# Two attention stages of a one-core transformer kernel: the output projection joined to the sparse attention, and single instructions moved up in the delta-rule stage

## What is computed

```
return jnp.concatenate([o, m], axis=-1) @ w_out        # second layer: o sparse attention, m memory attention
...
sol = lax.linalg.triangular_solve(lhs, rhs, left_side=True, lower=True, unit_diagonal=True)
u, w = sol[..., :Dv], sol[..., Dv:]
...
v_new = u_i - jnp.einsum('bhcd,bhde->bhce', w_i, S)    # per chunk of the delta rule, S is the state
...
z = jnp.einsum('bqhd,bkhd->bhqk', q[:, start:end], k[:, :end]).astype(jnp.float32) * scale
...
tail = lax.cumsum(log_one_minus, axis=3, reverse=True) - log_one_minus
A = jnp.where(strict, jnp.exp(log_beta + tail), 0.0)   # stick-breaking
```

## Time and profile before

| what | us |
|---|---|
| median of 3 runs (1991.64 to 1992.54) | 1992.03 |
| time of the profiled execution | 1987.48 |
| its span in the trace | 1985.8 |
| PE busy, 10461 matmuls | 1920.5 |
| DVE busy | 1125.8 |
| ACT busy | 731.7 |
| POOL busy | 181.7 |

### The profile page before, as it was taken

One profiled execution on the slowest core, in us unless ns is written; L12 is line 12 of the kernel. 1 busy time (PEld: TensorE's weight loads), 2 busy tenths in 40 slices (PEclk: granted clock), 3 DMA queues, 4 the chain that ended last, 5 costly groups with the idle time before them and its releaser, 6 DMA issues. The chain is left out here.

```text
span 1985.8 us, 27212 instructions
## 1 busy us (share of the span) xinstructions
PE 1920.5 (97%) x10461; PEld 1574.5 (79%) x10461; DVE 1125.8 (57%) x1633; ACT 731.7 (37%) x1152; POOL 181.7 (9%) x179
## 2 busy tenths in 40 slices
PE   8999999999999998999999999999988999999998
PEld 7788788888788876668888878888777788888786
DVE  6435565566435547735665553558655567777533
ACT  7442542222324436624222232424643442222322
POOL 2201020000002004401000000200141020000001
PEclk9999999999999999999999999999999999999999
DMA  7311223332323520023323322242010223322331
GB/s 240 126 45 44 75 85 100 102 95 85 106 96 82 142 80 1 1 85 106 96 85 106 98 93 95 65 117 85 11 44 2 83 77 102 110 85 85 106 96 43
DMA packets 138567, 167.73 MB, mean 84 GB/s; under 512 B 28354, under 2 KB 106727, under 8 KB 138471
## 3 DMA queue, kind: packets, MB, share of 16 engines
q1 hardware_dynamic: 138291, 166.37, 27.3%
q10 hardware_dynamic: 180, 0.05, 0.0%
HBM read 164.29 MB, written 2.10 MB: 84 GB/s over the span
## 5 line engine op out<-in xcount | busy, mean ns | idle before, releaser
L195 PE MATMUL bank<-h_hi,w_hi 128*128 128x512 f32 x2192 | 860.1, 392 | 15.1 <-DVE h_lo L1666 6.3
L196 PE MATMUL bank<-h_lo,w_hi 128*128 128x512 f32 x2192 | 853.8, 390 | 0.0
L197 PE MATMUL bank<-h_hi,w_lo 128*128 128x512 f32 x2192 | 853.7, 389 | 0.0
L142 DVE TENSOR_TENSOR w_lo<-raw,w_hi 128x1024 fp32r<-128x1024 f32 x274 | 334.4, 1236 | 561.0 <-ACT w_hi L136 560.6
L195 PEld LDWEIGHTS bank<-h_hi,w_hi 128*128 128x128 f32 x2192 | 411.8, 188 | 109.5 <-issue 13.9
L136 ACT CAST w_hi<-raw 128x1024 fp32r<-128x1024 f32 x274 | 283.9, 1047 | 575.8 <-PE bank L195 569.2
L197 PEld LDWEIGHTS bank<-h_hi,w_lo 128*128 128x128 f32 x2192 | 411.9, 188 | 86.3
L196 PEld LDWEIGHTS bank<-h_lo,w_hi 128*128 128x128 f32 x2192 | 412.0, 188 | 85.9 <-issue 2.2
L1562 ACT ACTIVATE scratch<-scratch 128x512 f32<-128x512 f32 x66 | 41.8, 633 | 250.8 <-DVE scratch L1627 250.8
L326 POOL TENSOR_TENSOR tail<-keep 128x512 f32<-128x512 f32 x7 | 9.8, 1395 | 1209.7 <-ACT keep L310 1193.6
L1627 DVE SCALAR_TENSOR_TENSOR scratch<-keep,vecs,scratch 128x512 f32<-128x512 f32 x88 | 66.2, 752 | 10.8 <-DVE scratch L1626 1.7
(11 more groups left out here) (466 smaller groups left out, 1832.0 us busy)
## 6 DMA issues: line engine op xcount, KB each, us to landing
raw<-in_w_up SPq DMA_DIRECT2D x176, 256.0 KB, 3.0
raw<-in_w_down SPq DMA_DIRECT2D x44, 512.0 KB, 3.2
raw<-in_w_ffn_up SPq DMA_DIRECT2D x88, 256.0 KB, 3.3
raw<-in_w_mix_in SPq DMA_DIRECT2D x24, 512.0 KB, 3.7
raw<-in_w_ffn_down SPq DMA_DIRECT2D x22, 512.0 KB, 3.5
raw<-in_w_mem_kv SPq DMA_DIRECT2D x16, 512.0 KB, 5.0
raw<-in_a_w_in SPq DMA_DIRECT2D x16, 512.0 KB, 3.7
raw<-in_a_w_out SPq DMA_DIRECT2D x8, 512.0 KB, 3.9
```

The costliest lines, as they stand in the source:

```text
L142: dve.tensor_tensor(k.w_lo[n % RING][:, :], k.raw[n % RING][:, :], k.w_hi[n % RING][:, :].bitcast(F32), ALU.subtract)\
L195: a = pe.matmul(out, sh, mh, start=first, stop=False)
L196: pe.matmul(out, sh, ml, start=False, stop=False)
L197: c = pe.matmul(out, sl, mh, start=False, stop=last)
```

## The change

No product and no elementwise operation is added or left out. Five things stand elsewhere:

1. `stage_out_projection` is gone, and its work stands inside the block of `stage_nsa`. Its first weight chunk (kk 0 and 1, 24 matmuls) stands inside head 3, behind `turn(3, 8)` and `values_sel`; the other three stand behind `values_mem(3)`. SP's loads for it stand in that block, too.
2. In head 0 of the sparse attention the memory scores' `lows(9)` stands behind `weigh_sel(0, 0)` on DVE, and `exps(9)` behind the first `copy_turned` on ACT.
3. In the delta stage `exponents(0, 0)` stands ahead of `softplus(0, 2)` and `softplus(0, 3)`.
4. `weights(0, 3)` stands ahead of `y_copy(8)` on ACT.
5. For the second pair `exponents(1, 0)` stands ahead of `softplus(1, 2)`; `softplus(1, 3)` behind the two instructions that negate the corner of the inverse (L3221); and `exponents(1, 3)` behind the first copy to `vn`.

```diff
-def pe_group(k, pe, t, tiles, h_from=None, aside=None, rstd_by=None, order=tuple(range(8)), bank_free=None):
+def pe_group(k, pe, t, tiles, h_from=None, aside=None, rstd_by=None, order=tuple(range(8)), bank_free=None,
+             ready=None, chunks=range(4)):
...
-            pe.wait_ge(k.h_ready.sem, k.h_ready.at(h_from + order.index(kk) + 1))
+            pe.wait_ge(k.h_ready.sem, k.h_ready.at(h_from + (ready or order).index(kk) + 1))
...
-    for c in range(4):
+    for c in chunks:
...
+    first = k.ring.took
+    ho = k.handoff = Handoff(k, rounded=8)
     with k.nc.Block() as blk:
+        @blk.sync
+        def _(sp):
+            stream(k, sp, first + 8)
+
...
+            def out_bank_free(i):
+                if i == 0:
+                    pe.wait_ge(zc_read, 8)
+                elif i == 2:
+                    pe.wait_ge(me_done, 16)
...
                     elif m == 8:
                         values_sel(j, (2, 3))
+                        if j == 3:
+                            pe_group(k, pe, 0, out_tiles, 0, bank_free=out_bank_free, ready=order, chunks=(0,))
...
             values_mem(3)
+            pe_group(k, pe, 0, out_tiles, 0, ready=order, chunks=(1, 2, 3))
+            pe.wait_ge(fin, 4)
+            pe.wait_ge(finm, 4)
+            pe_group(k, pe, 4, out_tiles)
...
-            for n in range(NB):
+            for n in range(9):
                 lows(n)
                 if n == 5:
                     coef_local(0)
             weigh_sel(0, 0)
+            lows(9)
             weigh_sel(0, 1)
...
+            out_projection_dve(k, dve, ho, gain, first)
...
+                    if j == 0 and m == 0:
+                        exps(9)
...
+            out_projection_act(k, act, ho, gain, first)
...
             weights(0, 2)
+            weights(0, 3)
             y_copy(8)
-            weights(0, 3)
...
             r_step(2, 1)
+            exponents(0, 0)
             softplus(0, 2)
             softplus(0, 3)
-            exponents(0, 0)
...
             r_step(5, 1)
+            exponents(1, 0)
             softplus(1, 2)
-            softplus(1, 3)
-            exponents(1, 0)
             for g in range(G2):
...
+            softplus(1, 3)
             exponents(1, 1)
...
-            exponents(1, 3)
             dve.wait_ge(u_out, 4)
             for c in range(C):
                 u = chunk(Vb)[:, :, c, :]
                 if c == 0:
                     dve.tensor_copy(vn[0][:, :, :], u).then_inc(vr, 1)
+                    exponents(1, 3)
```

More of the change, by code:

```diff
@@ L1954, in stage_nsa_in, with stage_nsa @@
     k.advance(sums_full=2, rstd_ready=2, h_rounded=8, h_ready=8, sq_ready=8, sq_added=1, tile_full=26, tile_free=26)
-def stage_nsa(k):
+def stage_nsa(k, gain):
     NB = 10
@@ L2098, in values_mem @@
                 mm.then_inc(om_full, 1)
+            def out_bank_free(i):
[3 more added lines that the diff above has]
+                    pe.wait_ge(me_done, 16)
+            out_tiles = [feature_tile(k, m * P) for m in range(4)]
             for n in range(NB):
@@ L2239, in _ @@
                                    minv[j].unsqueeze(2).broadcast_to([P, 4, 256]), ALU.mult).then_inc(pm_ready, 1)
+            pool_sums(k, pool, ho, range(1, 4), 7)
         @blk.scalar
@@ L2299, in _ @@
             act_split(k, act, value, None, tiles=order[6:8])
-    k.advance(h_rounded=8, h_ready=8)
+            out_projection_act(k, act, ho, gain, first)
+    k.advance(tile_full=8, tile_free=8, h_rounded=8, h_ready=8)
 def mixed_chunks(k, w, parts):
```

33 lines of the change are left out of this document (1 added, 32 removed).

## The result

The change makes the kernel faster: 1975.61 us, median of 4 runs (1974.03 to 1979.41), against 1991.84 (1991.43 to 1992.54) for the kernel before in the same series; ratio 0.9921, 95% interval 0.9908 to 0.9933. The gain is 16.2 us.

What follows compares the result with a forecast made beforehand. PE's waits in the two touched stages, and half-clock stretches behind them, were taken as the bound. Terms 3.0 + 0.6 + 2.9 + 4.1 + 1.4 = 12.0 us, off the median 1992.03, gave 1980.0; range 1976.5 to 1985.5.

Steps and rivals of the forecast that it cites:

- Term 1: End of sparse attention: the joined output projection hides PE's wait ahead of the second chunk; 3.0 us gained.
- Term 2: Head 0: moving `lows(9)` removes only DVE's idle 0.58 us from the path; 0.6 us gained, 2.9 more if clock recovers.
- the first rival: Head 0: the clock also stays up, 2.9 us more, 14.9 in all, 1977.1 us; chance 0.12.
- the port rule: Head 0: DVE and POOL share an exclusive port lock; the moved instruction could lose up to 1.09 us, a 0.5 loss.
- Terms 3 and 4: Delta stage: `exponents(0, 0)` moved up gains 2.9 us; `weights(0, 3)` moved up gains 4.1, of which 1.65 is clock.
- Term 5: Delta stage, second pair: the 1.07 us wait goes, but `w_lo` leaves only 0.3 of the 2.13; 1.4 us gained.
- the clock takes part back: Delta stage: slow stretches in dense work cost 1.7 to 3.4 us of the gain, 1981.7 to 1983.4; chance 0.18.
- the last line of the sum: Whole kernel: median lies 4.55 us above the profiled execution; carried over, 1992.03 less 12.0 gives 1980.0 us.
- the cases below 1988: Whole kernel: outcomes counted as faster, below 1988 us; chances put at 0.93, lowered to 0.91 for the unseen.

Runs made afterwards that it cites:

- e2_head0: Kernel before with only `lows(9)` moved behind `weigh_sel(0, 0)` and `exps(9)` behind the first copy in head 0; 1990.37 us against 1992.62, ratio 0.9992.
- e9_before_half_filled: Kernel before in its old order, with 4, 3, 5, 2 and 2 unused matmuls in PE's idle times; 1982.89 us against 1992.15, ratio 0.9955.

## Why the prediction was wrong, point by point

**Term 1, 3.0:** measured 3.1, no wait in the second chunk; alone with its clock time 6.5. **Term 2, 0.6:** to the second turn it was 0.55. In the profiled pair the stretch behind it was half as long, 1.4 more, so the first rival came half true there. The moved L2151 took 0.17 us, like L2170 in the same place before, so the port rule of the Trainium skill ("SBUF — State Buffer", section "SBUF: two separate sides") showed no price here.

**Terms 3 and 4, 7.0:** up to the transposes behind `stick_values(0)` it was 1505.62 - 1441.29 = 64.33 us and is 1494.33 - 1437.09 = 57.24, 7.1 less. The waits left, 1.88 and 1.26, answer to the forecast of 1.9 and 1.5. Step by step from the stage's first product: `stick_tails(0, 2)` comes 3.0 us earlier (41.24 and 38.24), `stick_values(0)` 5.5 (59.37 and 53.86), and the last 1.6 are the half-clock stretch behind it that is gone. So both terms are right in their parts.

**Term 5, 1.4:** the 1.07 is gone. From the row at which the compared piece ends (1528.64, now 1520.89) to the first L2897 (1541.43 in the earlier trace rows, now L2884 at 1531.38) it is 2.3 us less, and from there to the projection 1.9 more: with the 1.07 that is 1.5 in all, on the chain through `w_lo` that the prediction described.

**The rival "the clock takes part back"** came true in the profiled execution, at another place and at a higher price than I gave (4.6 us instead of 1.7 to 3.4), behind waits so short that I had not thought of them. It isn't the gaps around `stick_tails(0, 1)` that did it: a stretch falls there in an execution of the old order, too (e2_head0). In the trace of the changed kernel the delta stage gained 7.1 - 4.6 + 1.5 = 4.0 us: from its first product to the projection it was 116.58 us and is 112.63.

**The step that failed** is the last line of the sum: "The median of the runs is 4.55 above it; I carry that over". It treated the difference as a constant beside the kernel. The rows divide the miss of 4.4 us (1980.0 - 1975.61) in two. With the new stretch's 4.6 put aside, the stages of the two traces differ by 5.07 + 7.09 + 1.47 = 13.6 us, 1.6 more than the sum, of which head 0's clock is 1.4. That gives 1987.48 - 13.6 = 1973.9, and the median is 1975.61: only 1.7 above it, where I had carried over 4.55. The 2.8 us between are the larger share of the miss. About 1.1 us of the 4.55 is the start, which the change doesn't touch. The rest is taken to be time at half clock behind the waits, which goes in part with them, as e9_before_half_filled shows. Carrying over nothing would have given 1975.5; that this fits is luck, since two errors of 1.6 and 1.7 cancel in it.

In sizes: the waits themselves gave 3.1 + 0.55 + 5.5 + 1.5 = 10.7 us in the traces, where the terms without the clock say 10.3. That leaves 5.5 of the 16.2 for the clock. The other way round, the mean clock rose by 6.3 thousandths, which at 1.0 us each (the table by clock) is 6.3, and at 9.3 / 7 = 1.3 each (e9_before_half_filled) 8. The waits were forecast well, and the clock was priced at 1.65 where it was worth 5.5 to 8.

The chances of the cases below 1988 add up to 0.94, not 0.93 as the prediction has it, which changes nothing.

**What stays open.** No trace of the kernel before at 0.988 exists here. The traces of the parts, at 0.991 to 0.994, show where such runs can lose time, but not how often each stretch falls. The parts alone add up to 21.7 and not 16.2; part of that can be noise (each is known to about 2 us), and I take it that parts 1 and 4 give back partly the same stretches, which is argued and not shown. Nor is it known what keeps the changed and filled kernels at 0.993 in some runs and 0.997 in others.

## What to carry to other kernels

Put the mean clock of the profiled execution beside those of the timed runs before you carry a difference between them over: a gap in the clock is time that the change may remove or bring. Compare also when the first stage that the change touches begins: here that start alone differed by 2.4 us between executions. Price an idle time of PE twice, once as the wait and once as the half-speed work behind it, and add the clock time as a range over many runs, not from the one stretch that a trace shows. To tell the two prices apart, fill the idle time with matmuls that nobody uses, and no longer than the wait: what the kernel gains is the clock's part. Look in the trace whether the filler really stands in the wait: behind it, it only adds work.

## What the runs showed of the hardware

- Where the clock falls differs between executions of the same instructions: at 12 to 20 us it was 1.00 in one and 0.57 in the other, and behind the 64 x 64 products of the delta stage, with 1.92 and 1.93 us busy of 3.10 ahead, 1.00 and 0.50.
- The stretches at half clock in the traces of this case were 3.4, 6.8 or 10.2 us long, the one at the program's end apart. Behind waits of only 0.39 and 0.80 us among small products one held for 10.2 us of dense work and cost 4.6.
- Matmuls that nobody uses made the kernel before 9.3 us faster, with every wait left in place.
- The time up to the first score product, with the same instructions, was 744.5 us in one execution and 746.9 in another, both at full clock; PE waited 0.77 and 2.06 us for one DMA.
- A matmul of two f32 operands, 128 x 512, takes nearly 0.9 us (7.03 / 8) and is two records in the trace; the split products of L195 to L197, of the same size, take 0.226 each.
